# Two-phase feed-forwards with products of 512 columns in a three-block transformer kernel

## The reference

```python
def _swiglu(h, w_gate_up, w_down):
    g, u = jnp.split(h @ w_gate_up, 2, axis=-1)      # [1024, 2 * 2816]
    return (jax.nn.silu(g) * u) @ w_down             # [2816, 1024]

for n in range(2):
    x = x + 0.5 * _swiglu(_rmsnorm(x, ffn1_norm[n]), ...)
    x = x + _hybrid_mixer(_rmsnorm(x, mix_norm[n]), ...)
    x = x + 0.5 * _swiglu(_rmsnorm(x, ffn2_norm[n]), ...)
x = _rmsnorm(x, final_norm)
```

## Time and profile before

| | us |
|---|---|
| median of 3 runs | 1714.05 |
| lowest, highest | 1714.02, 1716.49 |
| the profiled execution | 1713.29 |
| its span in the trace | 1711.5 |
| mean granted clock of TensorE, as a share of full speed | 0.977 |

### The profile page before, as it was taken

The page is one execution under the profiler, slowest core; times in us unless marked ns, Lnnn a source line. Parts: engine busy times, 40 slices in busy tenths (PEclk is TensorE's granted clock), DMA queues, the critical chain, the costliest instruction groups (busy, mean ns, idle before and its releaser), DMA issues.

```text
span 1711.5 us, 34742 instructions
## 1 busy us (share of the span) xinstructions
PE 1567.6 (92%) x14632; PEld 1389.5 (81%) x14633; DVE 870.4 (51%) x1465; ACT 631.2 (37%) x910; POOL 247.7 (14%) x215
## 2 busy tenths in 40 slices
PE   8999987776776677999999999999999999999998
PEld 8889964443333343999999899999999998999998
DVE  5875641111111111865568466555755577575554
ACT  6464321110000001543345554333533356553332
POOL 1120030000000000111114511111211117311110
PEclk9999989999889989999999999999999999999999
DMA  8543699999999999354567544555455566445551
GB/s 330 203 171 125 256 388 428 429 428 428 429 428 429 428 428 427 144 185 181 185 257 247 184 149 177 186 185 186 171 186 186 185 256 245 171 149 185 185 185 62
DMA packets 42639, 435.83 MB, mean 255 GB/s; under 512 B 5082, under 2 KB 5210, under 8 KB 7842
## 3 DMA queue, kind: packets, MB, share of 16 engines
q1 hardware_dynamic: 41858, 430.08, 64.1%
q0 software_dynamic: 672, 4.15, 0.6%
HBM read 431.05 MB, written 3.16 MB: 254 GB/s over the span
## 4 chain that ended last, share of the span: by engine, by line
PE 73%; SPq 10%; DMA 7%; DVE 5%; ACT 2%; issue 2%; POOL 0%; ACTq 0%; DVEq 0%
PE bank L678 20%; PE bank L680 20%; PE bank L679 20%; SPq L455 9%; DMA ring<-moe_w_dram 6%; PE bank L1061 3%; PE bank L1085 2%; PE bank L1012 1%; DVE lo_last L1900 1%; PE bank L1226 1%; ACT w_hi L1606 1%; PE bank L1245 1%; PE bank L726 1%; PE bank L1231 0%; DMA h_t<-area 0%
## 5 line engine op out<-in xcount | busy, mean ns | idle before, releaser
L678 PE MATMUL bank<-h_hi,w_hi 128*128 128x256 f32 x1964 | 558.3, 284 | 2.8 <-DVE h_lo L1891 1.8
L679 PE MATMUL bank<-h_lo,w_hi 128*128 128x256 f32 x1792 | 505.6, 282 | 0.0
L678 PEld LDWEIGHTS bank<-h_hi,w_hi 128*128 128x128 f32 x1964 | 370.6, 189 | 9.2 <-issue 5.4
L679 PEld LDWEIGHTS bank<-h_lo,w_hi 128*128 128x128 f32 x1792 | 338.2, 189 | 0.1
L680 PE MATMUL bank<-h_hi,lo_last 128*128 128x256 f32 x1172 | 330.6, 282 | 0.0
L1606 ACT CAST w_hi<-ring 128x2048 fp32r<-128x2048 f32 (+1 forms) x120 | 227.9, 1901 | 61.6 <-PE bank L680 51.4
L680 PE MATMUL bank<-h_hi,lo_first 128*128 128x256 f32 x792 | 223.3, 282 | 0.0
L680 PEld LDWEIGHTS bank<-h_hi,lo_last 128*128 128x128 f32 x1172 | 221.1, 189 | 0.0
L679 PE MATMUL bank<-hid_lo,w_hi 128*128 128x256 f32 x704 | 198.7, 282 | 0.0
L678 PE MATMUL bank<-hid_hi,w_hi 128*128 128x256 f32 x704 | 198.7, 282 | 0.0
L590 POOL TENSOR_TENSOR area<-area,stat 128x256 f32<-128x256 f32 x88 | 106.0, 1205 | 623.4 <-ACT area L1658 623.4
(11 more groups left out here) (427 smaller groups left out, 2643.9 us busy)
## 6 DMA issues: line engine op xcount, KB each, us to landing
ring<-layer_w_dram SPq DMA_DIRECT2D x120, 1536.0 KB, 6.3
ring<-moe_w_dram SPq DMA_DIRECT2D x88, 1536.0 KB, 36.9
area<-moe_w_dram SPq DMA_DIRECT2D x40, 1536.0 KB, 37.0
ring<-first_w_dram SPq DMA_DIRECT2D x21, 1536.0 KB, 6.2
bias_copies_dram<-bias_rows_dram POOLq DMA_DIRECT2D x1, 2048.0 KB, 9.8
h_t<-area SPq DMA_DIRECT2D x32, 64.0 KB, 3.3
ring<-first_w_dram SPq DMA_DIRECT2D x3, 512.0 KB, 6.7
x_t<-x_dram SPq DMA_DIRECT2D x1, 1024.0 KB, 5.1
```

The lines of the kernel that those rows point to most:

```text
L678: pe.matmul(out_ap, a_hi, b_hi, start=start, stop=False, **flags)
L679: pe.matmul(out_ap, a_hi, b_lo, start=False, stop=False, **flags)
```

## The change

- The slots are packed anew. GU_SLOTS = 15 slots hold the gate and up blocks of all 22 chunks, 24 blocks each, so a chunk covers two thirds of a slot; 8 more slots hold down, one output block with its 22 hidden blocks (2816 columns) each. A feed-forward has 23 slots in place of 22. The mixer's slots are transferred only as wide as they are used.
- PE runs gate_up for all 22 chunks, then `down(j)` for the 8 output blocks. All 22 hidden chunks are kept on chip as hi and lo pairs, in areas that the mixer and attention leave free (`hid_split`).
- A product is two matmuls. W_hi is loaded once and H_hi and H_lo, now side by side in `h_split`, stream as 512 columns into a whole bank; W_lo H_hi (256 columns) is added to the bank's first half.
- Gate and up of a chunk now fill two banks, whose halves must be added: ACT copies the second halves to SBUF (`copy_halves`, 512 elements), DVE adds the first halves (512), then scales gate; POOL scales up in place of silu's result.
- ACT makes hi for chunk c+4 and DVE lo for chunk c+3 while they handle chunk c. In the down phase `ffn_update` adds a pair's two halves to x (two steps) after every second output block, and the next stage's splits of x follow at once. The last sums of squares go between the last output blocks (`last_sums`).

```diff
-MIX_AT = CHUNKS
+GU_SLOTS = -(-CHUNKS * 2 * KB // PER_SLOT)
+FFN_SLOTS = GU_SLOTS + KB
+MIX_AT = FFN_SLOTS
 FFN2_AT = MIX_AT + MIX_SLOTS
-LAYER_SLOTS = FFN2_AT + CHUNKS
+LAYER_SLOTS = FFN2_AT + FFN_SLOTS
...
-        GATE_BANKS = ((0, 1, 2, 3), MIXED_BANKS)
+        GATE_BANKS = (4, 6, 0, 2)
+        FIRST_GATE_BANKS = (2, 0, 4, 6)
+        DOWN_BANKS = (0, 2, 4, 6)
+        FIRST_DOWN_BANKS = (4, 6, 0, 2)
...
+                cols = slice(0, slot_width(q))
+                sp.dma_start(ring[:, PLACES[at], cols], layer_w[q][:, cols]).then_inc(layer_full[at], 16)
...
-                    pool.wait_ge(S("silu_done"), n + 1)
-                    sg = gated[:, n % 2, :]
-                    pool.tensor_tensor(sg, sg, stat[:, 3, :], ALU.mult).then_inc(S("silu_scaled"), 1)
+                    pool.wait_ge(S("gate_scaled"), n + 1)
+                    up = gate_pair[:, n % 2, 1, :]
+                    pool.tensor_tensor(up, up, stat[:, 3, :], ALU.mult).then_inc(S("up_scaled"), 1)
...
+                gate_banks, down_banks = (FIRST_GATE_BANKS, FIRST_DOWN_BANKS) if value == 1 else (GATE_BANKS, DOWN_BANKS)
                 def gate_up(c):
-                    q, bank = at + c, GATE_BANKS[f][c % 4]
-                    pe.wait_ge(S("lo_a_ready"), FIRST_SPLIT + q + 1)
+                    first_bank = gate_banks[c % 4]
                     if c >= 4:
-                        pe.wait_ge(S("hid_made"), first_chunk + c - 3)
+                        pe.wait_ge(S("halves_summed"), first_chunk + c - 3)
...
                     order = [(side, k) for side in range(2) for k in range(KB)]
                     for side, k in sorted(order, key=lambda n: n[1]) if c == 0 else order:
+                        q, at_block = gate_up_place(at, c, side, k)
...
-                        m = weight_product(half(bank, side), q, (side * KB + k) * P, h_hi[:, k, :], h_lo[:, k, :],
-                                           start=side == k == 0, stop=k == KB - 1, skip_group_check=True)
+                        cols = slice(at_block, at_block + P)
+                        pe.matmul(halves(first_bank + side), hi_of(q)[:, cols], h_split[:, :, k, :],
+                                  start=k == 0, stop=False, skip_group_check=True)
+                        m = pe.matmul(half(first_bank + side, 0), lo_of(q)[:, cols], h_hi[:, k, :],
+                                      start=False, stop=k == KB - 1, skip_group_check=True)
...
+                    m.then_inc(S("b_used" if c % 3 == 2 else "a_used"), 1)
+                def down(j):
+                    q, to = at + GU_SLOTS + j, down_banks[j // 2] + j % 2
+                    pe.wait_ge(S("lo_a_ready"), FIRST_SPLIT + q + 1)
+                    last_in = max(c for c in range(CHUNKS) if gate_banks[c % 4] == down_banks[j // 2])
+                    pe.wait_ge(S("halves_summed"), first_chunk + last_in + 1)
+                    for c in range(CHUNKS):
+                        if j == 0:
+                            pe.wait_ge(S("hid_made"), first_chunk + c + 1)
+                        cols = slice(c * P, (c + 1) * P)
+                        pe.matmul(halves(to), hi_of(q)[:, cols], hid_split(c), start=c == 0, stop=False,
+                                  skip_group_check=True)
+                        m = pe.matmul(half(to, 0), lo_of(q)[:, cols], hid_split(c)[:, 0, :], start=False,
+                                      stop=c == CHUNKS - 1, skip_group_check=True)
                     m.then_inc(S("a_used"), 1)
-                def down(c):
-                    q, n = at + c, first_chunk + c
-                    pe.wait_ge(S("lo_b_ready"), ffn_slots(q))
-                    pe.wait_ge(S("hid_made"), n + 1)
-                    for j in range(KB):
-                        m = weight_product(half(4 + j // 2, j % 2), q, (2 * KB + j) * P, hid_hi[:, n % 3, :],
-                                           hid_lo[:, n % 3, :], start=c == 0 and j % 2 == 0, stop=c == CHUNKS - 1,
-                                           skip_group_check=True)
...
-                gate_up(0)
-                gate_up(1)
-                for c in range(2, CHUNKS):
+                for c in range(CHUNKS):
                     gate_up(c)
-                    down(c - 2)
-                down(CHUNKS - 2)
-                down(CHUNKS - 1)
+                for j in range(KB):
+                    down(j)
+                    if value == 3 * LAYERS and j and j % 2 == 0:
+                        last_sums(j // 2 - 1)
...
+                def copy_halves(c):
+                    n = CHUNKS * (2 * layer + f) + c
+                    first_bank = (GATE_BANKS if at else FIRST_GATE_BANKS)[c % 4]
+                    chunk_done(act, at, c)
+                    if n >= 2:
+                        act.wait_ge(S("hid_made"), n - 1)
+                    act.copy(gate_pair[:, n % 2], bank[:, first_bank:first_bank + 2, T:2 * T])\
+                        .then_inc(S("halves_copied"), 1)
+                if f:
+                    mixed_tokens_hi(value, at - 1)
                     table_for_root()
+                if f or not at:
+                    hi_b(at)
+                    hi_b(at + 1)
                 hi_a(at + 2)
-                hi_b(at)
                 if at:
                     norm_root(value, ACT.Silu)
                 else:
...
                 for c in range(CHUNKS):
                     n = CHUNKS * (2 * layer + f) + c
+                    copy_halves(c)
                     act.wait_ge(S("gate_scaled"), n + 1)
-                    sg = gated[:, n % 2, :]
+                    sg = gate_pair[:, n % 2, 0, :]
                     act.activation(sg, sg, ACT.Silu).then_inc(S("silu_done"), 1)
...
+                    if c + 4 < CHUNKS:
+                        hi_parts(at, c + 4)
+                    elif c != CHUNKS - 3:
+                        hi_a(at + GU_SLOTS + (0, 0, 1, 2)[c + 4 - CHUNKS])
                     if not at and RESIDUAL_AT <= c < RESIDUAL_AT + PAIRS:
                         second_norm_made(c - RESIDUAL_AT)
+                if value < 3 * LAYERS:
+                    table_for_root()
+                for j in range(KB):
+                    if j < KB - 1:
+                        hi_a(at + GU_SLOTS + 3 + j)
+                        if f and j >= KB - 3:
+                            hi_b(at + GU_SLOTS + 3 + j)
+                    if j % 2:
+                        p = j // 2
+                        if value < 3 * LAYERS:
+                            pair_hi(value + 1, p)
...
+            def ffn_update(value, at, p):
+                a_part_used(dve, at + GU_SLOTS + 2 * p + 1)
+                first_bank = (DOWN_BANKS if at else FIRST_DOWN_BANKS)[p]
+                xb = x_t[:, 2 * p:2 * p + 2, :]
+                own(stt(xb, bank[:, first_bank:first_bank + 2, 0:T], 0.5, xb, ALU.mult, ALU.add))
+                stt(xb, bank[:, first_bank:first_bank + 2, T:2 * T], 0.5, xb, ALU.mult, ALU.add)\
+                    .then_inc(S("x_updates"), 1)
...
                     squares_summed(value)
-                    lo_a(at + 2)
+                    if f:
+                        lo_b(at + 1)
                     own(rms_factor(value))
                 else:
                     first_factor()
                 for c in range(CHUNKS):
-                    n, bank = CHUNKS * (2 * layer + f) + c, GATE_BANKS[f][c % 4]
-                    dve.wait_ge(S("a_used"), sum(i % LAYER_SLOTS != FFN2_AT - 1 for i in range(at + c + 1)))
-                    sg, hid = gated[:, n % 2, :], hidden[:, n % 2, :]
-                    tt(sg, ps[bank][:, 0:T], stat[:, 3, :], ALU.mult).then_inc(S("gate_scaled"), 1)
+                    n = CHUNKS * (2 * layer + f) + c
+                    first_bank = (GATE_BANKS if at else FIRST_GATE_BANKS)[c % 4]
+                    dve.wait_ge(S("halves_copied"), n + 1)
+                    both, sg, hid = gate_pair[:, n % 2], gate_pair[:, n % 2, 0, :], gate_pair[:, n % 2, 1, :]
+                    tt(both, bank[:, first_bank:first_bank + 2, 0:T], both, ALU.add).then_inc(S("halves_summed"), 1)
+                    dve.wait_ge(S("halves_summed"), n + 1)
+                    tt(sg, sg, stat[:, 3, :], ALU.mult).then_inc(S("gate_scaled"), 1)
                     if f == 0 and c == 4:
                         layer_constants(layer)
...
+                    if c + 3 < CHUNKS:
+                        lo_parts(at, c + 3)
+                    elif c != CHUNKS - 2:
+                        lo_a(at + GU_SLOTS + (0, 0, 1)[c + 3 - CHUNKS])
+                    dve.wait_ge(S("silu_done"), n + 1)
+                    dve.wait_ge(S("up_scaled"), n + 1)
+                    own(tt(hid, sg, hid, ALU.mult))
+                    hid_hi, hid_lo = hid_split(c)[:, 0, :], hid_split(c)[:, 1, :]
+                    own(dve.tensor_copy(hid_hi, hid))
+                    tt(hid_lo, hid, hid_hi.bitcast(F32), ALU.subtract).then_inc(S("hid_made"), 1)
                     if not at and RESIDUAL_AT <= c < RESIDUAL_AT + PAIRS:
```

(14 more changed lines are left out.)

229 lines of the change are left out of this document (137 added, 92 removed).

## The result

The changed kernel takes 1705.2 us (median of 6 runs, 1703.6 to 1708.3) against 1714.9 us for the kernel before (median of 6, 1712.5 to 1716.5): a ratio of 0.9947, with a 95% interval from 0.9934 to 0.9960. It is faster, as predicted, but by 10 us and not by 44: the time lies 11 us above the upper end of the range. The profiled execution has a span of 1703.0 us against 1711.5, which leaves 8.5 us to explain.

A forecast was written before the change was run, and what follows sets the result against it. From 696.6 us on PE's stream of matmuls was taken as the bound. Terms -48.6 + 0.25 + 1.9 + 1.7 - 1.0 + 2.0 = -43.7 us gave 1670.3 us; own range 1662 to 1679, whole range 1647 to 1694 (87 in 100).

The forecast's parts named there:

- part 1: 2112 weight-block products of four feed-forwards: each falls from 358.5 to 335.5 ns (216 + 119.5), 48.6 us gained.
- first feed-forward's opening and chunks 9 to 12: First feed-forward: 0.25 us lost at the opening, and PE waits 1.9 us near chunks 9 and 10.
- second feed-forward's openings, two: Second feed-forward, twice: PE waits 0.85 us for part b of slot 0, 1.7 us lost in all.
- openings behind a down phase: Both mixers and the second layer's first feed-forward: only x's last pair is outstanding, 1.0 us gained in all.
- tail: Kernel's end: sum passes between output blocks, then updates, square and passes behind the last product; net 2.0 us lost.
- The narrow step: 256-column matmul on PE: 119.5 ns, a weight load plus some 10 ns of handover, with the stream hidden in it.
- The rival in which it takes 109: Rival: the 256-column step behind a wide one takes 109 ns, the load's own pace; 1648.1 us, 10 in 100.
- The wide step that costs more: Rival: the 512-column step costs 226 ns, 13 over its stream; 1692.5 us, 13 in 100.
- The serial chunks: Rival: ACT's copy waits for all of the chunk before, 8.3 us a chunk; 1925 us, 3 in 100.
- the chain over ACT, DVE and POOL as the pace of the phase: Rival, gate-up phase: copy and POOL wait add to DVE's 4.53 us, 5.78 a chunk; 1706 us, 5 in 100.
- the 512 columns run as two times 256: Rival: each half runs at a load's pace, a product stays 358.5 ns; 1718.9 us, 4 in 100.
- Wide matmuls that overlap beyond their stream: Rival: a 512-column step takes 167 ns, a product 287; 151 us gained, 1519 us, 1 in 100.

The follow-up runs named there:

- m4_passes: A kernel of its own, streaming rounded steps and unrounded fp32 passes on TensorE alone: 228.6 ns per rounded 512-column step, 216 per unrounded pass of 256.
- e4: The changed kernel with GpSimd's scaling of up cut to 16 of 256 columns, the rest left unscaled: 1700.28 us, ratio 0.9924 to the kernel before.
- e5: The changed kernel with VectorE scaling gate and up in one step, GpSimd's scaling removed: 1701.38 us, ratio 0.9928 to the kernel before.
- e1: The changed kernel with each 512-column matmul issued as two of 256, each with its own load: 1714.75 us, ratio 1.0006 to the kernel before.

## Why the prediction was wrong

**The failed step** is in part 1, "I take 216 because its row has the same stream and a load in it". The row, is a pass of unrounded fp32. m4_passes measured that pass at 216 again, with 2.7 ns over its stream, and the rounded step of 512 columns at 228.6. The duration was right and the analogy wrong: the same stream does not make the same step. The upper bound that I gave for it, 226, was the better number; it took its overhead (13 ns) from the rounded 256-column step of the same kernel. Even that was 3 to 7 ns short of 228.7 alone and 233 in turn. I gave it 13 in 100 against 64.

With the measured 352 ns the first term is 2112 x 5.9 = -12.5 us, from 189.0/528 = 358 ns before, and not -48.6. This term alone is 36 us off, the whole of the error. The other terms, read from the profiled executions against it:

| term | forecast | measured |
|---|---|---|
| products, four feed-forwards | -48.6 | -12.5 |
| first feed-forward's opening and chunks 9 to 12 | +2.15 | +2.2 (190.20 to 189.34, less 3.1 for its products) |
| second feed-forward's openings, two | +1.7 | +1.3 (2 x (187.07 - 189.50 + 3.1)) |
| openings behind a down phase | -1.0 | -1.7 (mixers 122.50 to 121.06 and 122.4 to 122.6; 0.5 in the second layer); -3.2 without the 1.5 us of low clock |
| tail | +2.0 | +2.2 (the last stage is 11.3 us longer than a second feed-forward before, 13.5 after) |
| sum | -43.7 | -8.5 (the spans differ by 8.5) |

The figures that the prediction took from the Trainium skill (TensorE: Matmul & The Clock Gate, Back-to-back issue gap) enter no term. Worked out, N/2.4 + 2.5 ns gives 3 x 109.2 - (109.2 + 215.8) = 2.5 ns a product, an estimate of 5 us for the change and not the 7 of the prediction.

**The narrow step** had the right size, 119 to 120 ns, and costs the same up to 264 columns. That it is the load's pace plus a handover is not borne out: it falls to 112.9 with 192 columns and to 113.7 with half the load. The rival in which it takes 109 was rightly put low.

**The waits** came where I had put them and nearly as large, at chunks 9 to 12 and in the openings, but not for the whole of the reason given. I wrote "POOL 1.20, under DVE's 2.29". The op lay under a split and was held up by it to 2.445 us (e4: 2.20 with a sixteenth of the columns), so VectorE waited for it 66 times, 47.3 us in all. The trace of the kernel before had shown it: its 1.20 us were held up already, by a split of 1024 columns. All 88 of these ops there start beside a split and end 0.6 us after it, as they do now (the median of the 84 that meet one):

```profile
1045.57 1.22 DVE L1908 TENSOR_TENSOR lo_first<-ring,w_hi 128x1024 fp32r<-128x1024 f32 x1
1046.18 1.20 POOL L590 TENSOR_TENSOR area<-area,stat 128x256 f32<-128x256 f32 x1 [7.34 <-ACT area L1658]
```

VectorE's chunk was 5.18 us and not 4.53. That TensorE's chunk was 5.63 and not 5.37 made up for some two fifths of it: a lead of 0.45 us a chunk, not 0.84. Two errors met, and that the term came out about right is luck: the 2.2 us of the table are net of waits that the kernel before had itself, and by e5 the waits of the first feed-forward cost 3.7 us. e4 and e5 show that without GpSimd's part the residual would have cost nothing at all.

**The tail** came out as worked: 0.69 + 0.69 for the two updates, 0.63 for the square, 1.05 as listed for the sums. It answers to the earlier trace rows:

```profile
1693.19 0.69 DVE L1984 SCALAR_TENSOR_TENSOR x_t<-bank,x_t 128x512 f32<-128x512 f32 x1
1693.92 0.63 ACT L1699 ACTIVATE sq<-x_t 128x512 f32<-128x512 f32 x1 [15.74 <-DVE x_t L1984]
...
1694.60 1.05 PE L1171 MATMUL bank<-consts,sq 128*128 128x1 f32 x8 [2.17 <-ACT sq L1699]
1695.69 0.16 DVE L2037 TENSOR_SCALAR r_tok<-bank 128x2 f32<-128x2 f32 x1 [1.81 <-PE bank L1171]
```

**The rivals.** The wide step that costs more was the right one, and nearly in size; whether its 13 ns are the same overhead as the narrow step's is not shown. Its time of 1692.5 was 13 us too low, since 226 was not 233 (7 x 2.112 = 15 us). The serial chunks, the chain over ACT, DVE and POOL as the pace of the phase, and the 512 columns run as two times 256 did not come: e1, which runs them so, is 5 ns a product slower. My point from which that rival's result would show, 237 ns, lay only 4 ns above what was measured. Wide matmuls that overlap beyond their stream show in no run. The range was set by two steps of 216 +- 10 ns, each of which I had bounded by rows of another kind. Of my own signs "a wide step over 220 ns" came true, and so did a granted clock below 1.00 after 700 us, but that one explains 1.5 us.

What stays open is why wide rounded steps pay these 13 to 20 ns. It isn't the change of weights, the rows, the banks, the place of the tokens or other engines' work; that is as far as these runs go. The load is not ruled out: every step in every stream carries its own, listed at 188 ns in rounded fp32 and at 98 in bf16, and no run streams rounded columns without one. Nor is it shown why a change between the two types costs 20 to 30 ns.

## What to carry to other kernels

Where two ways of issuing differ by ten nanoseconds an instruction, take the overhead from a row of the same type, and not from one that merely streams as long; if there is none, the range must hold the larger overhead of either. Joining two matmuls into one wide one saves the part of a step that the stream did not cover, here 119 + 119 - 233 = 5 ns, and not the weight load. And an op on GpSimd is not hidden by a VectorE op that reads two SBUF operands: it gets on only when that op ends, so giving VectorE the work itself, 0.27 us more, gained 3.7 us in the first feed-forward. A measured duration of such an op is no price of its own: look first at what ran beside it.

## What the runs showed of the hardware

- Rounded fp32 steps on TensorE, in a stream at the upper clock: 109.5 ns for 128 columns, 112.9 for 192, 120 for 256 and 264, then 11 to 12 ns over columns/2.4 GHz up to 304 and 13 to 20 from 320 to 512, whether the weights change or not and with 64 rows as with 128. Dense bf16: 2.5 ns over it. Unrounded fp32, per pass of 256 or 512 columns: 2.3 to 2.7 ns over twice the columns/2.4 GHz.
- A bf16 step of 256 columns takes 109.2 ns with dense operands and 113.4 with operands read from the upper halves of fp32 words.
- In a mixture of rounded and bf16 steps the bf16 ones save little: 358 ns a pair in turn, where single streams of dense operands would give 338; with upper halves 346 in groups of 8 and 343 in groups of 16, where they would give 342.
- GpSimd on 16 columns took 2.20 us beside a VectorE split of 2.29 us, and 0.22 without one; on 256 columns it ended 0.6 us after a split whether that took 1.22 or 2.29 us, and took 0.74 without one.
- TensorE went on at a granted clock of 0.52 after a stop of 4.8 us. After stops of 2.45 us it had 1.00 in one kernel and 0.58 in another. In a mixer, with TensorE busy throughout, it fell to 0.83 over 10 us (1460 to 1470) in one profile of the changed kernel and stayed at 1.00 in the other.
